# Attention's value products with the queries as stationary side

## The reference

```python
def attend(q_nope, q_rope, k_nope, k_rope, v):
    s = (jnp.einsum('bqhd,bkhd->bhqk', q_nope, k_nope)
         + jnp.einsum('bqhr,bkr->bhqk', q_rope, k_rope)).astype(jnp.float32) * SOFTMAX_SCALE
    p = jax.nn.softmax(s, axis=-1).astype(v.dtype)
    return jnp.einsum('bhqk,bkhd->bqhd', p, v)

def merge_groups(conv_out, attn_out, w_o, b_o):
    b, n = conv_out.shape[:2]
    cat = jnp.concatenate([conv_out, attn_out.reshape(b, n, N_HEADS * V_DIM)], axis=-1)
    return cat @ w_o + b_o
```

## Time and profile before

| what | value |
|---|---|
| median of three runs | 1128.92 us |
| the profiled execution's own time | 1131.28 us |
| its span | 1129.5 us |
| PE busy | 1089.3 us, 96% |
| DVE busy | 793.4 us, 70% |
| ACT busy | 547.2 us, 48% |
| POOL busy | 78.2 us, 7% |

### The profile page before, as it was taken

One profiled execution on the slowest core, in us unless ns is written; L12 is line 12 of the kernel. 1 busy time (PEld: TensorE's weight loads), 2 busy tenths in 40 slices (PEclk: granted clock), 3 DMA queues, 4 the chain that ended last, 5 costly groups with the idle time before them and its releaser, 6 DMA issues.

```text
span 1129.5 us, 14930 instructions
## 1 busy us (share of the span) xinstructions
PE 1089.3 (96%) x5947; PEld 890.6 (79%) x5947; DVE 793.4 (70%) x1285; ACT 547.2 (48%) x961; POOL 78.2 (7%) x115
## 2 busy tenths in 40 slices
PE   3899999999999999999999999999999999999996
PEld 3678888888888888888867666779888888888885
DVE  5776898877677846667897899786666566645246
ACT  3566655666333447764256675455444444432121
POOL 1020011111321000100000002000000000000001
PEclk9899999999999999999999999899999999999999
DMA  9644233444265663131010211032323232352301
GB/s 378 264 185 151 97 131 148 149 169 168 85 220 208 252 224 127 48 133 61 28 49 1 75 44 69 1 112 84 106 109 103 84 112 79 109 191 89 112 1 75
DMA packets 22510, 136.40 MB, mean 121 GB/s; under 512 B 2560, under 2 KB 2856, under 8 KB 8616
## 3 DMA queue, kind: packets, MB, share of 16 engines
q1 hardware_dynamic: 19936, 128.46, 31.0%
q10 hardware_dynamic: 2504, 6.98, 1.8%
HBM read 133.32 MB, written 2.12 MB: 120 GB/s over the span
## 4 chain that ended last, share of the span: by engine, by line
PE 90%; DVE 5%; ACT 3%; DMA 1%; issue 1%; POOL 0%; DVEq 0%; SPq 0%; ACTq 0%; POOLq 0%
PE PB L185 88%; PE PB L193 1%; ACT WH L199 1%; DMA XL<-in_x 1%; DVE WL L206 1%; DVE XL L214 1%; DVE EARLY L1410 1%; ACT PTA L200 0%; ACT HH L199 0%; DVE XL L218 0%; DVE HL L206 0%; DVE CV L214 0%; DVE RAW L1410 0%; ACT YG L197 0%; ACT HB L200 0%
## 5 line engine op out<-in xcount | busy, mean ns | idle before, releaser
L185 PE MATMUL PB<-HH,WH 128*128 128x512 f32 (+1 forms) x896 | 346.1, 386 | 11.1 <-DVE HL L206 6.8
L185 PE MATMUL PB<-HH,WL 128*128 128x512 f32 (+1 forms) x896 | 340.3, 380 | 0.0
L185 PE MATMUL PB<-HL,WH 128*128 128x512 f32 (+1 forms) x896 | 340.1, 380 | 0.0
L206 DVE TENSOR_TENSOR WL<-RAW,WH 128x1024 fp32r<-128x1024 f32 (+2 forms) x172 | 197.4, 1153 | 192.4 <-ACT WH L199 192.0
L199 ACT ACTIVATE WH<-RAW 128x1024 fp32r<-128x1024 f32 (+2 forms) x172 | 167.7, 980 | 286.2 <-PE PB L185 267.5
L185 PEld LDWEIGHTS PB<-HH,WH 128*128 128x128 f32 x896 | 169.1, 189 | 47.3 <-DVE HL L206 7.5
L185 PEld LDWEIGHTS PB<-HH,WL 128*128 128x128 f32 x896 | 169.2, 189 | 32.0
L185 PEld LDWEIGHTS PB<-HL,WH 128*128 128x128 f32 x896 | 169.4, 189 | 30.0 <-issue 0.2
L214 DVE SCALAR_TENSOR_TENSOR CV<-VP,PC,CV 128x512 f32<-128x512 f32 x120 | 88.0, 778 | 0.7
L185 PE MATMUL PB<-WH,AL 128*128 128x512 f32 x176 | 68.6, 390 | 0.0
L185 PE MATMUL PB<-WH,AH 128*128 128x512 f32 x176 | 68.5, 389 | 0.0
(11 more groups left out here) (284 smaller groups left out, 1681.1 us busy)
## 6 DMA issues: line engine op xcount, KB each, us to landing
RAW<-in_wstream SPq DMA_DIRECT2D x101, 1024.0 KB, 4.8
EARLY<-in_wstream SPq DMA_DIRECT2D x7, 1024.0 KB, 15.1
RAW<-in_wstream SPq DMA_DIRECT2D x5, 768.0 KB, 4.2
RAW<-in_wstream SPq DMA_DIRECT2D x5, 512.0 KB, 3.4
XL<-in_x SPq DMA_DIRECT2D x2, 1024.0 KB, 8.0
HB<-in_x SPq DMA_DIRECT2D x2, 1024.0 KB, 6.0
out<-XL SPq DMA_DIRECT2D x8, 256.0 KB, 2.0
ROWS<-in_rows ACTq DMA_DIRECT2D x3, 512.0 KB, 7.6
```

The source lines that it names most:

```text
L185: return self.put(lambda e: e.matmul(o, l, r, start=start, stop=stop, skip_group_check=skip))
L206: return self.put(lambda e: e.tensor_tensor(o, a, b, op))
```

## The change

The value products turn round. The stationary side is now 64 queries of the exponentials, the moving side 65 columns: the 64 value columns of a head and one column of ones. The two halves of the PE array (columns 0 to 63 and 64 to 127) take turns with the two halves of each 128 queries. So a head's result stands with the queries on the partitions, four blocks of 65 columns in one bank, and each divisor is one column. Instead of one product for each key tile, three key tiles are taken at a time, 24 products in a row: `values(h, 0)` in step 3 of head h, and `values(h, 1)` in step 0 of the next head. The exponentials have five buffers.

DVE takes the reciprocal of the four divisor columns (`divisors`, in step 1 of the next head); ACT copies the values out, scaled by it, in four pieces of 64 columns (`values_out`, which waits for the reciprocal). Logarithm, exponential and the product `pair` are gone. When both heads of a pair are there, PE turns them back with four transposes (`turned_pair`, step 3 of heads 2, 4, 6 and, for the last pair, inside the first block of the projection), and ACT and DVE make high and low halves from PSUM. `pair_high` and `pair_low` of pair 2 move into step 4 and step 5 of head 6.

```diff
@@ -490,9 +490,9 @@
-    PR = [PTA[:, 512 * i:512 * i + 512] for i in range(3)]
+    PR = [z[:, 512 * i:512 * i + 512] for z, n in ((PTA, 3), (TMP, 2)) for i in range(n)]
+    RCP = SCT[:, 48:56]
@@ -1220,35 +1220,25 @@ (act_prog)
             a.wait_ge(S_.p_sm, ("s", h, t))
-            if s > 2:
-                a.wait_ge(S_.p_sm, ("o", (s - 3) // 6, (s - 3) % 6))
-            a.act(PR[s % 3], main.of(("s", h, t)), ACTF.Exp, scale=SCALE).then_inc(S_.a_ev, ("s", h, t))
+            if s > 4:
+                a.wait_ge(S_.p_sm, ("o", (s - 5) // 6, (s - 5) % 6 // 3))
+            a.act(PR[s % 5], main.of(("s", h, t)), ACTF.Exp, scale=SCALE).then_inc(S_.a_ev, ("s", h, t))
 
         def values_out(h):
-            me, other = ((0, 64), (64, 128)) if h % 2 == 0 else ((64, 128), (0, 64))
-            z = aux.of(("ov", h))
-            a.wait_ge(S_.p_sm, ("o", h, 5))
-            i = h // 2 % 2
-            if h > 3:
-                a.wait_ge(S_.v_h, ("m", 4 + h // 2 - 2))
-            a.copy(OTS[i][me[0]:me[1], :], z[me[0]:me[1], :])
-            a.copy(SU[i][me[0]:me[1], :], z[other[0]:other[1], :]).then_inc(S_.a_ax, ("ov", h))
-
-        def divisors(*pairs, between=None):
...
+            o, z, p = OTS[h // 2 % 2], aux.of(("ov", h)), h // 2
+            a.wait_ge(S_.v_s, ("rcp", h))
+            if p > 1:
+                a.wait_ge(S_.p_sm, ("ot", p - 2))
+            for i in range(4):
+                c = 65 * i + h % 2
+                op = a.act(o[:, 128 * i + 64 * (h % 2):128 * i + 64 * (h % 2) + 64], z[:, c:c + 64], ACTF.Identity,
+                           scale=RCP[:, 4 * (h % 2) + i:4 * (h % 2) + i + 1])
+            op.then_inc(S_.a_ax, ("ov", h))
 
         def pair_high(p):
-            a.wait_ge(S_.v_s, ("pair", p))
-            a.copy(MH[:, 4 + p, :], OTS[p % 2]).then_inc(S_.a_h, ("m", 4 + p))
+            a.wait_ge(S_.p_sm, ("ot", p))
+            a.copy(MH[:, 4 + p, :], aux.of(("ot", p))).then_inc(S_.a_h, ("m", 4 + p))
@@ -1893,13 +1880,18 @@ (dve_prog)
-        def pair(p):
-            v.wait_ge(S_.a_s, ("su", p))
-            v.tt(OTS[p % 2], OTS[p % 2], SU[p % 2], MUL).then_inc(S_.v_s, ("pair", p))
+        def divisors(h):
+            c = 64 * (1 - h % 2)
+            z = aux.of(("ov", h))[:, 0:260].rearrange("p (i n) -> p i n", n=65)[:, :, c:c + 1].rearrange("p i n -> p (i n)")
+            v.wait_ge(S_.p_sm, ("o", h, 1))
+            if h > 1:
+                v.wait_ge(S_.a_ax, ("ov", h - 2))
+            v.recip(RCP[:, 4 * (h % 2):4 * (h % 2) + 4], z).then_inc(S_.v_s, ("rcp", h))
@@ -1917,6 +1909,8 @@
         for h in range(8):
             for t in range(6):
+                if t == 1 and h:
+                    divisors(h - 1)
                 if 1 <= t <= 4 and h < 7:
                     maxima(h + 1, t - 1)
...
-                if t == 0 and h in (3, 5):
-                    pair_low((h - 3) // 2)
+                if t == 5 and h in (2, 4, 6):
+                    pair_low(h // 2 - 1)
...
                 conv((h, t))
@@ -2487,13 +2477,32 @@ (pe_prog)
-        def values(h, t):
-            bk = take_aux(("ov", h), 2 + h % 2) if t == 0 else aux.of(("ov", h))
...
-            pe.mm(bk, VG[:, t, c:c + 128], PR[(6 * h + t) % 3], t == 0, t == 5).then_inc(S_.p_sm, ("o", h, t))
+        def values(h, part):
...
+            c = 192 * (h // 2) + 127 * (h % 2)
+            for t in range(3 * part, 3 * part + 3):
+                pe.wait_ge(S_.a_ev, ("s", h, t))
+                p = PR[(6 * h + t) % 5]
+                for i in range(4):
+                    for n in range(2):
+                        q = 128 * i + 64 * n
+                        op = pe.mm(bk[64 * n:64 * n + 64, 65 * i:65 * i + 65], p[:, q:q + 64], VG[:, t, c:c + 65],
+                                   t == 0 and i == 0, t == 5 and i == 3, True)
+            op.then_inc(S_.p_sm, ("o", h, part))
+
+        def turned_pair(p):
+            bk = take_aux(("ot", p), 3 if p < 3 else 2)
+            pe.wait_ge(S_.a_ax, ("ov", 2 * p + 1))
+            for i in range(4):
+                op = pe.tr(bk[:, js(i)], OTS[p % 2][:, js(i)], IDN[:, :])
+            op.then_inc(S_.p_sm, ("ot", p))
@@ -2509,10 +2518,12 @@
                 scores(h, t)
-                if t:
-                    values(h, t - 1)
-                elif h:
-                    values(h - 1, 5)
+                if t == 3:
+                    if h in (2, 4, 6):
+                        turned_pair(h // 2 - 1)
+                    values(h, 0)
+                elif t == 0 and h:
+                    values(h - 1, 1)
                 if 1 <= t <= 4 and h < 7:
                     maxima(h + 1, t - 1)
@@ -2546,7 +2557,10 @@
+            if n == 0:
+                rows(ys, B_O + n, merged(k), True, False, (0, 1), False)
+                turned_pair(3)
-            rows(ys, B_O + n, merged(k), n == 0, n == 3, (2, 3) if n == 1 else range(4))
+            rows(ys, B_O + n, merged(k), n == 0, n == 3, (2, 3) if n < 2 else range(4))
```

More of the change, by code:

```diff
@@ L373, in build_in @@
     S_ = Sems(nc, ctx)
-    EV, AX = (S_.a_ev, S_.v_ev), (S_.a_ax, S_.v_ax, S_.v_s)
+    EV, AX = (S_.a_ev, S_.v_ev), (S_.a_ax, S_.v_ax, S_.v_s, S_.v_h)
     IDN = sb("IDN", [128, 128])
@@ L492, in build_in @@
     VG = sb("VG", [128, 6, 768], F32, c2)
-    SU = [TMP[:, 512 * i:512 * i + 512] for i in range(2)]
     CKH, CKL = (z[:, 3:6, :].rearrange("p a n -> p (a n)").rearrange("p (k n) -> p k n", n=NKEY) for z in (CH, CL))
-    PR = [PTA[:, 512 * i:512 * i + 512] for i in range(3)]
+    PR = [z[:, 512 * i:512 * i + 512] for z, n in ((PTA, 3), (TMP, 2)) for i in range(n)]
+    RCP = SCT[:, 48:56]
     VGs = VG[:, :, :].rearrange("p t (a s n) -> p t a s n", a=4, s=3)
@@ L1276, in act_prog @@
                 power_of(h, t)
-                if t == 2 and h in (2, 4):
-                    divisors(h // 2 - 1)
                 if t == 0 and h % 2 and h < 6:
@@ L1284, in act_prog @@
                     maxima(h + 1, t - 1)
-                if t == 5 and h in (2, 4):
+                if t == 4 and h in (2, 4, 6):
                     pair_high(h // 2 - 1)
@@ L1301, in act_prog @@
                         conv_square(j)
-        a.wait_ge(S_.p_sm, ("o", 7, 5))
+        values_out(7)
+        a.wait_ge(S_.p_sm, ("o", 7, 1))
         a.wait_ge(S_.vec, "g2")
@@ L1305, in act_prog @@
             a.dma(row, VEC[1 + n:2 + n, :].partition_broadcast(128)).then_inc(S_.row, *["o"] * n, by=16)
-        values_out(7)
         def last_squares():
@@ L1312, in last_squares @@
             split(B_O + NW)
-        divisors(2, 3, between=last_squares)
-        pair_high(2)
+        last_squares()
         pair_high(3)
@@ L1927, in dve_prog @@
                     split(KEY_BLOCK[(h + 1) // 2] + NW)
-                if t == 4 and h in (2, 4):
-                    pair(h // 2 - 1)
                 if t == 3 and h < 6:
@@ L1943, in dve_prog @@
         cm, cv_, cr, cq_ = (CNT[:, 4 * i:4 * i + 4] for i in range(4))
+        divisors(7)
         conv("end")
         split(B_O + NW)
-        for p in (2, 3):
-            pair(p)
         st = aux.of("cvs")
@@ L1955, in dve_prog @@
         v.tt(cv_, cv_, cq_, SUB).then_inc(S_.v_s, "nv")
-        for p in (2, 3):
-            pair_low(p)
+        pair_low(3)
         v.wait_ge(S_.g_s, "npw")
@@ L2488, in scores @@
             pe.mm(bk, ONESR, DGR[h % 2][:, :], False, True).then_inc(S_.p_sm, ("s", h, t))
-        def values(h, t):
-            bk = take_aux(("ov", h), 2 + h % 2) if t == 0 else aux.of(("ov", h))
+        def values(h, part):
+            if part == 0:
+                bk = take_aux(("ov", h), 2 + h % 2)
+            else:
+                bk = aux.of(("ov", h))
             pe.wait_ge(S_.g_s, "vone")
             pe.wait_ge(S_.a_ev, ("v", h // 4, 2))
-            pe.wait_ge(S_.a_ev, ("s", h, t))
-            c = 192 * (h // 2) + 64 * (h % 2)
-            pe.mm(bk, VG[:, t, c:c + 128], PR[(6 * h + t) % 3], t == 0, t == 5).then_inc(S_.p_sm, ("o", h, t))
+            c = 192 * (h // 2) + 127 * (h % 2)
[14 more added lines that the diff above has]
+            op.then_inc(S_.p_sm, ("ot", p))
         query(0)
@@ L2525, in pe_prog @@
                     keys(h // 2 + 1, (2 + n % 2, 3 - n % 2))
-        values(7, 5)
+        values(7, 1)
         def conv_sums():
```

11 lines of the change are left out of this document (2 added, 9 removed).

## The result

The changed kernel takes 1138.17 us (median of four runs, 1135.15 to 1140.88) against 1128.83 (1128.21 to 1130.1) of the kernel before on the same chip: a ratio of 1.0078 [1.0059, 1.0097]. Forecast were 1132.8 us and a range up to 1137.5. The direction was right, the size was not, and the time lies just outside the range.

What follows compares the result with a forecast made beforehand. PE was taken to bound the attention's first half and share the second with DVE. -4.5 (S) + 5.6 (stall) + 0.45 (last transposes) + 2.3 (clock) = +3.9 us: 1135.2 profiled, 1132.8 median; range 1128.0 to 1137.5.

Steps and rivals of the forecast that it cites:

- the price of a group: PE's 48 passes for three key tiles: 1.84 us instead of 2.58, saving 0.74 in each of 16 groups, 11.8 in all.
- The nearest row: Profile row of 16 passes, 64 stationary and 64 moving columns, alternating array halves: 0.031 us a pass, used for 1.84.
- the stall behind S: Head 7: PE waits 7 us for exponentials queued behind head 6's copy-out and reciprocal; projection 5.6 us later.
- S: Start of row maximum (7, 3), at 686.24 us in the kernel before; forecast to come 4.5 us earlier.
- a third fall of the clock: In PE's new idle time in head 7 its clock halves, costing 1.5 to 3.2 us, taken as 2.3.
- the copy of the last pair: Before the last transposes: the copy is done before PE finishes 12 products (2.7 us), so only 0.45 us counts.
- How much of it arrives at S: Walk from row maximum to row maximum, each step the later of PE and DVE: 4.5 us gained, bounds 2 and 11.
- the level of the median: The median of the runs lies 2.36 us below the profiled execution, so 1135.2 becomes 1132.8.
- The clock doesn't fall: Rival: the stall in head 7 comes but the clock holds; +1.6 us, 1130.5; chance 0.14.
- the halves don't overlap: Rival: array halves fail to overlap in the value products, 2.9 us a group; about +12, 1141; chance 0.08.
- The saving arrives: Rival: all DVE idle time ahead of S goes; -2.7 us, 1126.2; chance 0.13 together with DVE reaching the reciprocal in time.
- the bunched group: Three key tiles between row maxima 1 and 2: 6.9 us from maximum 0 (6.5 without transposes), before 6.3 to 6.4.

Runs made afterwards that it cites:

- the second trace of the changed kernel: The changed kernel run again, unedited, on another chip: 1137.05 us, ratio 1.0062 to the kernel before.
- The first experiment: Late copy-out: the changed kernel with ACT's copy-out of head 6 moved behind the exponentials of head 7; 1136.61 us, ratio 1.0052 to the kernel before.
- the fourth: The changed kernel with 28 unread products of 512 columns put where PE waits in head 7; 1136.19 us, ratio 1.0046 to the kernel before.
- The short taps: Attention's 88 convolution taps cut to 8 columns: kernel before 1130.43 us, changed kernel 1127.25, the repaired one 1123.18.
- the repaired one: Changed kernel with head 6's copy-out behind head 7's exponentials, heads 0-6's first group and transposes in step 4, head 7's reciprocal six taps earlier; 1129.64 us, ratio 0.9996.
- the spread taps: The repaired one with the convolution taps distributed anew over the steps of even and odd heads; 1127.32 us, ratio 0.9963 to the kernel before.
- group in step 4: The changed kernel with the first group and the transposes moved from step 3 to step 4 in heads 0 to 6; 1136.31 us, ratio 1.0055.

## Why the prediction was right and wrong

**Right: the price of a group.** Forecast 1.84 us, 0.0315 a pass. The first group of head 0:

```profile
586.49 0.40 PE L185 MATMUL PB<-DGR,HH 128*128 128x512 f32 x1
586.82 1.62 PE L185 MATMUL PB<-VG,PTA 128*64 128x65 f32 x48
588.37 0.62 PE L185 MATMUL PB<-KH,HH 128*128 128x512 f32 x2
588.83 0.39 PE L185 MATMUL PB<-HH,KH 128*128 128x512 f32 x1
```

The product ahead of it holds PE for 0.23, and the one behind it starts at 588.37, which makes 1.65. The first product behind it takes 0.46 for its two parts (588.83 - 588.37), where 0.35 is usual (580.06 to 580.41), so with leaving the mode the group costs 1.76; a pass is (1.62 - 0.22) / 47 = 0.030. The nearest row was the right one. The Trainium skill ("TensorEngine Tiling (Array Packing)", Theoretical Speedup) has up to a factor of two for halves of the columns. Here 2.58 us of full-width products became 48 x 0.030 = 1.44 us of passes, a factor of 1.8, and with 0.32 for going in and out 1.5.

**Right: the stall behind S.** Forecast: reciprocal at S + 12.0, four copies of 0.28, PE idle for 7 us from S + 7.5, a third fall of the clock that costs 1.5 to 3.2, projection at S + 18.9 and with the clock S + 21.2. Measured: reciprocal at S + 11.4, the four copies 0.93 together, idle for 6.05 us until S + 13.6, 3.2 us lost at half clock, projection at S + 20.75. The two terms were 5.6 + 2.3 = 7.9, and 7.5 came, with some luck: the wait was 1 us too long in the forecast and the clock's part 0.9 too small. In the second trace of the changed kernel the same wait cost 6.05 in all, since the clock fell later. The first experiment shows that this wait is the cause, and the fourth that the clock's part is real.

**Wrong in passing: the copy of the last pair "is done".** In the changed kernel the stall hides it. With the stall gone it costs 5.35 us, because the reciprocal of head 7 is queued behind 18 taps.

**Wrong: the step "How much of it arrives at S".** Forecast -4.5, measured +0.1. Row maximum (5, 0) was to gain 3.7 and gained 74.83 - 73.88 = 0.95 behind (0, 0); the rest of the way lost 1.1. Two numbers of my walk were too small. For the stretch from maximum 0 to maximum 2 I had 6.9 with transposes and 6.5 without; it is 7.2 (613.83 to 621.06) and 6.8 (582.25 to 589.03), and 7.15 where DVE makes the low keys (597.66 to 604.81, 0.4 of it a wait for them): 0.3 to 0.65 more, 3.0 in seven heads. And for 2 to 3 I had 1.48, where the loop takes 1.67 in the five heads that have nothing else there: 0.95. From the start of a maximum to the product that it releases are 1.01 us (582.25 to 583.26), where I had 0.88, and from the product to the next maximum 0.66 (588.37 to 589.03), where I had 0.35; both numbers were too small. Together this is 3.9 of the 4.6 that were missed. The other 0.7 is what is left of larger amounts: row maxima (2, 2) to (2, 3) and (3, 2) to (3, 3) lie 2.7 us apart, and not 1.48, because PE makes products for the values of later heads between them (before 3.55, which my "1.66 to 2.14" left out), and the stretches from 3 to the next 0 became 2.0 us shorter in sum, where I had taken off 0.3 (2 x 0.6 - 6 x 0.15).

The deeper fault is the rule that I built on, that a faster PE is worth DVE's idle time. That idle time (8.9 and 3.6 us after the change) is no stock from which a saving is paid: 7.1 of the 12.5 us are waits in the bunched stretch, 1 to 2, while PE's own waits for row maxima lie behind maxima 0 and 2, the longest 1.76 us ahead of 583.26. The short taps show it plainly. With DVE free, the changed order still gives 3.2 us and the repaired one 7.2; 1.6 of this difference is the wait in head 7, the rest the place of the group.

**Wrong by the sample: the level of the median.** I took 2.36 off, since the three runs known of before lay that far below its profiled run. On other chips its medians were 1130.48 to 1131.24, and the changed kernel's median lay 1.04 above its profiled run. In the profiled executions the miss is 1137.13 - 1135.2 = 1.9 us: 4.6 at S, -0.4 in head 7, -1.6 behind it, -0.7 at the start. The other 3.4 are this. Times of one kernel follow the mean granted clock of the run: of nine runs of the changed kernel the two at 0.991 took 1134.4 and 1134.5 us, those at 0.986 to 0.988 1139.2 to 1140.9. The profiled one had 0.990.

**The rivals.** "The clock doesn't fall" is refuted by the clock rows, "the halves don't overlap" by the group of 1.55. "The saving arrives" named the bunched group as what stood against it. That is so, but moving the group was not enough (nothing at the projection), and only with the spread taps does a part of the saving arrive, 4.4 us.

**Open.** Why the fall in the one-column products lasts 3.4 us in one trace and 6.8 in another, and is missing in a third, was not settled; 3.4 us of it are worth 1.7. Nor was it settled why three traces of edited kernels (late copy-out, group in step 4, repaired) have a fall near 585 us, behind a wait of PE of 1.8 us that the changed kernel has as well without a fall. It was not tried to give the row maxima a second pair of banks, which might open the loop of 1.67.

## What to carry to other kernels

A saving on the engine that binds arrives only where its neighbours' order lets the next step start earlier: walk the loop stretch by stretch with both queues, sum the distances of a marker that repeats (here the row maxima), and do not treat idle time of the other engine as a sum to be spent. When small products are bunched, look at which step becomes the longest, and move the other engine's filler work out of the steps that became short and into those that became long. And when a copy-out starts to depend on another engine, go through both queues to every place where its result is needed, the last one too. Three moves, two of them such places, were worth 7 us here. A mark such as S must have the same work ahead of it in all kernels that it compares.

## What the runs showed of the hardware

- Products on alternate column halves start 0.030 us apart with 65 float32 columns, four in a row on the same half and then four on the other (2.12 - 0.22) / 47 = 0.040 on the average. That is far from twice as long; whether products on one half overlap in part as well, no run told.
- A tap takes 0.66 us alone (five in 3.39 us). Nine taps behind S took 9.00 us in the changed kernel, where three of POOL's sums ran beside them, and 10.20 in the repaired one, where all four did. The Trainium skill ("SBUF — State Buffer", Who interferes with whom) says that a DVE instruction with two SBUF inputs contends with a GpSimd instruction that reads SBUF, for a shared pair of ports that is an exclusive lock. The slower taps agree with it: in the trace of before four taps beside the sums took 6.68 us, 1.67 each.
